# Two decoder layers: from a two-pass loop with barriers to one straight program, with the normalization folded into the product that turns x

## The chip, the cores and the metric

The kernel runs on one core of a Trainium2 chip. The metric is the device time of one execution in microseconds (us), the median of several runs. The engines are TensorE (PE, with its weight loads as PEld), VectorE (DVE), ScalarE (ACT), GpSimd (POOL) and SyncE (SP), which issues nearly all transfers.

## The reference

Two residual layers over x of 256 tokens by 1024 features, all in float32, and one closing normalization:

```
for l in range(2):
    h = x * rsqrt(mean(x*x) + 1e-6) * norm_g[l]
    proj = h @ w_in[l]                     # 1024 x 10008
    y_lru, y_s5, y_ret, y_nsa = four causal mixers of slices of proj
    ys = [y * silu(gate_path)]             # four times 256 x 512
    merged = sum(sigmoid(merge_n) * (ys_n @ w_branch[l, n]))
    x = x + merged @ w_out[l]
return x * rsqrt(mean(x*x) + 1e-6) * final_norm_g
```

The S5 mixer is a diagonal state-space recurrence. Its coefficients come from small per-layer parameter vectors by exponentials, sines and cosines, on tiles of 128x16.

## The kernel before

A layer is one list of 36 `CHUNKS`, each a product of 256 tokens with up to 512 output columns. The weights come in 74 units of two K-tiles through a ring of four tiles `raw` (`load_unit`, issued by SP). The twelve chunks named in `NATIVE` multiply `raw` in full float32, each such product leaving two records on PE. The others are split: ACT copies `raw` to `w_hi` (`cast_units`), POOL subtracts to `w_lo` (`split_lo`), and PE makes three products of rounded parts. The order of the work on every engine is written out by hand: PE calls `chunk(...)` and, in between, the small products of the mixers (`state_inputs(p)` and `state_outputs(p)` for the S5 mixer); DVE runs `angles(p)` and `scan_pair(p)` for the eight S5 pairs.

**Prologue** (L454 to L494). A block of its own: SP loads `x` whole, the constants, 13 small parameter rows (`load_vectors`) and two weight units. ACT makes the squares of x (`squares`, L438), DVE and POOL the inverse root `st[:, 2:4]` (`mean_square`, `inverse_root`), PE turns the parameter rows into columns (`turn_vectors`, L428) and DVE keeps them in `vec` (`keep_vectors`). The block ends with a barrier of all engines.

**Layer** (L496, a hardware loop of two passes). DVE scales x by the inverse root into `merged` (L844). PE transposes it in sixteen 128x128 pieces (L1322) into the bank tile `M`, ACT scales the pieces by `norm_g` into `h_full` and rounds `h_hi`, DVE subtracts `h_lo` (L863). Then comes the chunk `u_s5` (L1367). Meanwhile DVE and ACT work out the S5 coefficients (L846 to L909), which the tiles `b_exp` need (L914 to L918) before PE can turn them after `u_s5`. At the end `out_0a`, `out_1a`, `out_0b` and `last_chunk()` make the output product: DVE adds its parts to x (L1308, L1313), ACT squares them (L438) for the next normalization. The parameter rows of the next layer and its first two weight units are loaded and turned already here.

**Between the passes.** The block of the layer ends with a barrier, a block of its own clears all semaphores (`sem_clear`) and the loop jumps back.

**Epilogue** (L1716 to L1728). A third block: DVE multiplies x, inverse root and `final_norm_g` for each half of the tokens (L1727), SP stores each (L1721).

Of the kernel before, what the change touches and what calls it, by code (L numbers as in the profile page):

```python
# [65 lines left out]
N_FIRST = 2  # L66
# [4 lines left out]
SPLIT_UNITS = [u for u in range(NU) if CHUNKS[UNITS[u][0]][0] not in NATIVE]  # L71


def splits(upto):
# [7 lines left out]
    0, 8, 24, 28, 32, 36, 40, 44, 52, 68, 96, 112)  # L82

# [59 lines left out]
def hybrid_trunk(nc, a, out):  # L143
# [4 lines left out]
    with ctx:  # L148
# [3 lines left out]
        sems = []  # L152

        def sem(name):
            sems.append(ctx.enter_context(nc.semaphore(name)))
            return sems[-1]
# [43 lines left out]
        sc = sb("sc", [P, 7168])  # L200
        half_pi = sb("half_pi", [P, 1])
# [67 lines left out]
        x_loaded, const_loaded = (ctx.enter_context(nc.semaphore(n)) for n in ("x_loaded", "const_loaded"))  # L269
# [7 lines left out]
        x_norm, xT_done = sem("x_norm"), sem("xT_done")  # L277
# [30 lines left out]
        STAGE = ("vectors_loaded", "raw_first", "dt_rows", "vecT", "vec_ready", "sq", "msq", "var", "rstd", "g_loaded")  # L308
        nxt = {n: sem("next_" + n) for n in STAGE}
        first = {n: ctx.enter_context(nc.semaphore("first_" + n)) for n in STAGE}  # L310
        normed, stored = (ctx.enter_context(nc.semaphore(n)) for n in ("normed", "stored"))
# [3 lines left out]
        for u, (c, _, _, _) in enumerate(UNITS):  # L315
            if u >= N_FIRST:
                _count[u % N_RAW] += 32 if c == CHUNK["cmp"] else 16
            raw_target.append(_count[u % N_RAW])
# [79 lines left out]
        def load_vectors(sp, l, signal):  # L398

            def load(dst, src):  # L400
                sp.dma_start(dst, src).then_inc(signal, 16)

            for name, at, n in (("norm_g", V_NORM, 8), ("lru_conv_w", V_CONV, 16), ("lru_conv_b", V_CONVB, 4),
                                ("lru_ba", V_BA, 4), ("lru_bx", V_BX, 4), ("lru_lambda", V_LAM, 4), ("s5_d", V_D, 4),
                                ("s5_b_glu", V_BGLU, 8), ("s5_lambda_re", V_LR, 16), ("s5_lambda_im", V_LI, 16)):
                src = a[name][l]
# [7 lines left out]
            load(dt_in[V_DT:V_ROWS, :], a["s5_log_dt"][l].rearrange("(s g) -> s g", g=2))  # L414
            for m, name in enumerate(("nsa_pos_k", "nsa_pos_v")):
                load(rows2[16 * m:16 * m + 16, :], a[name][l].rearrange("(r s) d -> r (s d)", s=2))

        VECTORS_ALL, RAW_ALL = 16 * 13, 16 * N_FIRST

        def expand_dt(stage):  # L420

            nc.vector.tensor_copy(rows[V_DT:V_ROWS, :].rearrange("p (g n) -> p g n", g=2),
                                  bc(dt_in[V_DT:V_ROWS, :].unsqueeze(2), [16, 2, 64])).then_inc(stage["dt_rows"], 1)

        def turn_vectors(stage):

            for dst, src, n in ((M[:, 0, 0:V_ROWS], rows[0:V_ROWS, :], V_ROWS), (M[:, 0, P:P + 32], rows2[:, :], 32)):
                nc.tensor.transpose(dst, src, ident[0:n, 0:n]).then_inc(stage["vecT"], 1)  # L428

        def keep_vectors(stage):  # L430

            nc.vector.tensor_copy(vec[:, :], M[:, 0, 0:V_ROWS])
            nc.vector.tensor_copy(flat(pos[:, :, :]), M[:, 0, P:P + 32]).then_inc(stage["vec_ready"], 1)

        def squares(stage, half, t):

            e = slice(512 * half, 512 * half + 512)
            nc.scalar.activation(merged[:, t, e], x[:, t, e], ACT.Square,  # L438
                                 accum_out=st[:, 4 + 2 * half + t:5 + 2 * half + t]).then_inc(stage["sq"], 1)

        def mean_square(dve, stage):

            dve.wait_ge(stage["sq"], 2 * TT)
            nc.vector.tensor_tensor(st[:, 0:2], st[:, 4:6], st[:, 6:8], ALU.add).then_inc(stage["msq"], 1)
            dve.wait_ge(stage["msq"], 1)
            nc.vector.tensor_scalar(st[:, 0:2], st[:, 0:2], 1.0 / D, EPS, ALU.mult, ALU.add).then_inc(stage["var"], 1)

        def inverse_root(gp, stage):

            gp.wait_ge(stage["var"], 1)  # L450
            nc.gpsimd.tensor_tensor(st[:, 2:4], st[:, 0:2], m_half[:, 0:2], ALU.pow).then_inc(stage["rstd"], 1)


        with nc.Block() as block:  # L454
            @block.sync
            def _(sp):
                sp.dma_start(x[:, :, :], a["x"][0].rearrange("(t p) d -> p t d", p=P)).then_inc(x_loaded, 16)
                sp.wait_ge(first["dt_rows"], 1)
                sp.dma_start(const[:, :], a["constants"]).then_inc(const_loaded, 16)
                load_vectors(sp, 0, first["vectors_loaded"])  # L460
                for u in range(N_FIRST):
                    load_unit(sp, u, 0, first["raw_first"])
                sp.wait_ge(first["raw_first"], RAW_ALL)

            @block.gpsimd
            def _(gp):
                gp.memset(half_pi[:, :], math.pi / 2)
                gp.memset(m_half[:, :], -0.5)
                gp.memset(wa[:], 0.0)
                gp.memset(wx[:], 0.0)  # L470
# [5 lines left out]
            def _(act):  # L476
                act.wait_ge(x_loaded, 16)
                for half in range(2):
                    for t in range(TT):
                        squares(first, half, t)  # L480
# [1271 lines left out]
```

## Time and profile before

| | |
|---|---|
| median of 3 runs | 883.88 us (882.99 to 884.66) |
| the profiled execution, its own time | 883.38 us |
| its span, first to last instruction | 881.6 us |
| PE busy | 824.0 us, 93% of the span |
| PEld, DVE, ACT, POOL busy | 608.4, 562.3, 312.9, 313.7 us |
| mean granted TensorE clock | 0.973 of full speed |
| instructions | 10702 |

Busy times are those of one profiled execution. A line of the timeline says when a group of instructions starts and how long it takes; brackets behind it give how long the engine had been idle and what ended that.

### The profile page before, as it was taken

Reading aid. Unit: us, or ns where it says so; the run is one execution under the profiler, and the core shown is the slowest. Engines: PE = TensorE matmul, PEld = TensorE weight load, DVE = VectorE, ACT = ScalarE, POOL = GpSimd, SP = SyncE. Lnnn points to the kernel's source line nnn. Section 1 sums busy time; section 2 is a strip of 40 time slices with the busy share of each in tenths; the row PEclk is TensorE's granted clock in tenths of the full one; section 3 lists DMA queues with packets and bytes.
Section 4 is the critical chain, followed back from the end, with each engine's and each line's share of the span. In section 5 each row is a group of like instructions: output and inputs, shape, how many; then the busy total and the mean of one; then the engine's idle time right before and its main releaser. Section 6 shows DMA issues by size and latency. Waiting matters only on the chain. (4 is left out here: it accounts for less than half of the span.)

```text
span 881.6 us, 10702 instructions
## 1 busy us (share of the span) xinstructions
PE 824.0 (93%) x3852; PEld 608.4 (69%) x3852; DVE 562.3 (64%) x937; ACT 312.9 (35%) x519; POOL 313.7 (36%) x134
## 2 busy tenths in 40 slices
PE   4999989999999799999879998999998989999995
PEld 3874764446878688888768556744477777888884
DVE  3888999464697652634268889964928974445342
ACT  5310212013743445464334112110164544555441
POOL 0000000005568576668400000000057676666872
PEclk9999999999999899999979999999999998999998
DMA  7575524445345444454255745344453344444551
GB/s 227 135 240 152 184 84 140 122 146 189 116 120 168 120 143 144 144 168 147 69 113 150 236 137 191 96 143 128 136 190 122 117 140 127 138 137 154 168 167 71
DMA packets 87507, 128.29 MB, mean 146 GB/s; under 512 B 22204, under 2 KB 32792, under 8 KB 87320
## 3 DMA queue, kind: packets, MB, share of 16 engines
q1 hardware_dynamic: 87448, 127.55, 46.5%
q8 instruction: 32, 0.52, 0.2%
q14 instruction: 27, 0.22, 0.1%
HBM read 126.48 MB, written 1.05 MB: 145 GB/s over the span
## 5 line engine op out<-in xcount | busy, mean ns | idle before, releaser
L560 POOL TENSOR_TENSOR w_lo<-raw,w_hi 128x1024 fp32r<-128x1024 f32 x120 | 307.0, 2588 | 534.1 <-ACT w_hi L576 503.1
L1371 PE MATMUL proj<-raw,h_full 128*128 128x512 f32 (+1 forms) x512 | 213.2, 572 | 0.0
L1371 PEld LDWEIGHTS proj<-raw,h_full 128*128 128x128 f32 x512 | 95.7, 190 | 104.5 <-issue 100.6
L576 ACT ACTIVATE w_hi<-raw 128x1024 fp32r<-128x1024 f32 x120 | 122.5, 1050 | 65.1 <-DMA raw<-in_s_w_glu 27.1
L1327 PE MATMUL proj<-w_hi,h_hi 128*128 128x512 f32 x320 | 128.7, 402 | 0.9 <-POOL w_lo L560 0.9
L1367 PE MATMUL proj<-h_full,raw 128*128 128x256 f32 x512 | 119.0, 393 | 7.5 <-DVE gate L978 7.5
L1327 PE MATMUL proj<-w_lo,h_hi 128*128 128x512 f32 x320 | 125.0, 391 | 0.0
L1327 PE MATMUL proj<-w_hi,h_lo 128*128 128x512 f32 x320 | 125.0, 391 | 0.0
L1367 PEld LDWEIGHTS proj<-h_full,raw 128*128 128x128 f32 x512 | 100.2, 198 | 23.1 <-DVE gate L978 7.9
L1327 PEld LDWEIGHTS proj<-w_hi,h_hi 128*128 128x128 f32 x320 | 60.1, 188 | 14.3 <-issue 1.7
L1327 PEld LDWEIGHTS proj<-w_hi,h_lo 128*128 128x128 f32 x320 | 60.1, 188 | 13.0
L1327 PEld LDWEIGHTS proj<-w_lo,h_hi 128*128 128x128 f32 x320 | 60.2, 188 | 11.9 <-issue 0.5
L1327 PE MATMUL proj<-w_hi,ys_hi 128*128 128x512 f32 x128 | 53.3, 416 | 5.2 <-POOL w_lo L560 5.1
L1327 PE MATMUL proj<-w_hi,ys_lo 128*128 128x512 f32 x128 | 51.8, 405 | 0.0
L1327 PE MATMUL proj<-w_lo,ys_hi 128*128 128x512 f32 x128 | 51.6, 403 | 0.0
L576 ACT ACTIVATE sc<-sc,st 128x256 f32<-128x256 f32 x64 | 28.2, 442 | 57.2 <-DVE st L1249 57.2
L1002 DVE SCALAR_TENSOR_TENSOR mt<-mt,proj 128x1024 f32<-128x1024 f32 x12 | 14.7, 1221 | 39.3 <-PE proj L1327 39.3
L576 ACT ACTIVATE mt<-proj 128x1024 f32<-128x1024 f32 x16 | 16.3, 1019 | 63.3 <-PE proj L1371 54.4
L576 ACT ACTIVATE sc<-sc 128x512 f32<-128x512 f32 (+2 forms) x38 | 23.5, 666 | 42.0 <-DVE sc L1090 37.4
L1327 PEld LDWEIGHTS proj<-w_hi,ys_hi 128*128 128x128 f32 x128 | 25.3, 198 | 11.8 <-issue 5.9
L1327 PEld LDWEIGHTS proj<-w_lo,ys_hi 128*128 128x128 f32 x128 | 25.5, 199 | 5.1
L1327 PEld LDWEIGHTS proj<-w_hi,ys_lo 128*128 128x128 f32 x128 | 24.9, 195 | 5.7
(283 smaller groups left out, 1194.6 us busy)
## 6 DMA issues: line engine op xcount, KB each, us to landing
raw<-in_w_in SPq DMA_DIRECT2D x154, 512.0 KB, 3.5
raw<-in_w_branch SPq DMA_DIRECT2D x32, 512.0 KB, 3.6
raw<-in_w_out SPq DMA_DIRECT2D x16, 512.0 KB, 3.7
raw<-in_s_w_glu SPq DMA_DIRECT2D x8, 512.0 KB, 3.6
raw<-in_w_in SPq DMA_DIRECT2D x8, 256.0 KB, 2.5
merged<-in_nsa_ck_w SPq DMA_DIRECT2D x4, 512.0 KB, 5.7
mt<-in_nsa_ck_w SPq DMA_DIRECT2D x4, 512.0 KB, 6.8
merged<-in_nsa_cv_w SPq DMA_DIRECT2D x4, 512.0 KB, 5.1
```

Of the source, the lines that this page charges most:

```text
L560: nc.gpsimd.tensor_tensor(w_lo[:, s % N_SPLIT, 0:n * w], raw[:, u % N_RAW, 0:n * w], w_hi[:, s % N_SPLIT, 0:n * w].bitcast(f32), ALU.subtr ...
L576: i = nc.scalar.activation(out_, in_, func, **kw)
L1002: v.scalar_tensor_tensor(m, m, 1.0, src, ALU.add, ALU.mult).then_inc(evac(full), 1)
L1327: last = mm(dst, left[i], right[j], start=start and n == 0, stop=stop and n == 2, skip_group_check=True)
L1367: last = mm(ps[:, m * T:(m + 1) * T], rw[:, m * P:(m + 1) * P], h_full[:, k, :], start=st_ and m % 2 == 0, stop=sp_, skip_group_check=True)
L1371: last = mm(ps[:, 512 * t:512 * t + w], h_full[:, k, t * P:(t + 1) * P], rw, start=st_, stop=sp_, skip_group_check=True)
```

## The change

1. The loop becomes a Python loop: both layers are written out in one block, without a barrier, `sem_clear` or jump. `Layer` adds to every awaited count what a layer has signalled before (`PER_LAYER`). The closing normalization is in the same block.
2. The normalization of x is not done by DVE any more. `scaled_identity` makes a 128x128 matrix with the inverse root on its diagonal, and `turn_x` multiplies the pieces of x by it, a full float32 product in place of a transpose, for each half of the tokens by itself.
3. The inverse root is made for each half of the tokens by itself.
4. `parameters(l + 1)`, the S5 coefficients and other small preparations, run on DVE and ACT at the end of layer l. `turn_vectors` stands ahead of `out_1a` in place of behind it. In the first layer `parameters(0)` stands behind the eight `h_full` on ACT.
5. `h_hi` is made after `trig(0)`, `h_lo` after `gate_times("lru")`; PE waits for `h_lo` ahead of `merge_s5_1`.
6. At the start x is loaded in halves with the identity between them, then the parameter rows, seven issued by SP and six by ACT, then two weight units, the other constants and two more units. At the layer boundary all four first units of the next layer are loaded ahead, and the tables `b_nat` and `c_nat` after the last transposes of the layer.
7. The closing normalization is made and stored in four pieces of 512 columns.

The new helpers, the start of the block, and SP at the start:

```diff
+        def mean_of_first_half(dve, l, link):
+            Layer(dve, l).wait_ge(sq, TT if l else 2 * TT)
+            link(nc.vector.tensor_scalar(st[:, 0:2], st[:, 4:6], 1.0 / D, EPS, ALU.mult, ALU.add))
+        def mean_square(dve, l, t):
+            Layer(dve, l).wait_ge(sq, TT + t + 1)
+            nc.vector.scalar_tensor_tensor(st[:, t:t + 1], st[:, 6 + t:7 + t], 1.0 / D, st[:, t:t + 1],
+                                           ALU.mult, ALU.add).then_inc(var, 1)
+        def inverse_root(gp, l, t):
+            Layer(gp, l).wait_ge(var, t + 1)
+            nc.gpsimd.tensor_tensor(st[:, 2 + t:3 + t], st[:, t:t + 1], m_half[:, 0:1], ALU.pow).then_inc(rstd, 1)
+        def scaled_identity(dve, l, t):
+            Layer(dve, l).wait_ge(rstd, t + 1)
+            nc.vector.tensor_scalar(diag[:, t, :], ident, st[:, 2 + t:3 + t], None, ALU.mult).then_inc(diag_done, 1)
+        def turn_x(pe, l, t):
+            Layer(pe, l).wait_ge(diag_done, t + 1)
+            for k in range(KD):
+                at = (k % 2) * T + t * P
+                last = nc.tensor.matmul(M[:, k // 2, at:at + P], x[:, t, k * P:(k + 1) * P], diag[:, t, :], start=True, stop=True)
+                if t == TT - 1 and k % 2:
+                    last.then_inc(xT_done, 1)
...
-        with nc.Fori(0, DEPTH) as l:
-            with nc.Block() as block:
+        with nc.Block() as block:
+            for l in range(DEPTH):
...
+                    if l == 0:
+                        queue.dma_start(x[:, 0, :], a["x"][0][0:P, :]).then_inc(x_loaded[0], 16)
+                        queue.dma_start(const[:, 0:P], a["constants"][:, 0:P]).then_inc(ident_loaded, 16)
+                        queue.dma_start(x[:, 1, :], a["x"][0][P:T, :]).then_inc(x_loaded[1], 16)
+                        sp.wait_ge(cleared, 1)
+                        load_vectors(queue, 0, VECTORS_A)
+                        prefetch(0)
+                        prefetch(1)
+                        queue.dma_start(const[:, P:N_CONST], a["constants"][:, P:N_CONST]).then_inc(const_loaded, 16)
```

ACT at the start of a layer:

```diff
+                    if l == 0:
+                        scalar.wait_ge(cleared, 1)
+                        load_vectors(scalar, 0, VECTORS_B)
+                        for t in range(TT):
+                            scalar.wait_ge(x_loaded[t], 16)
+                            for half in range(2):
+                                squares(half, t)
+                    act.wait_ge(vec_ready, 1)
                     for k in range(KD):
                         if k % 2 == 0:
                             act.wait_ge(xT_done, k // 2 + 1)
                         run(h_full[:, k, :], M[:, k // 2, (k % 2) * T:(k % 2 + 1) * T], ACT.Copy, hfull_done,
                             scale=vec[:, V_NORM + k:V_NORM + k + 1])
-                        if k % 2:
-                            act.wait_ge(hfull_done, k + 1)
-                            run(flat(h_hi[:, k - 1:k + 1, :]), flat(h_full[:, k - 1:k + 1, :]), ACT.Copy, hhi_done)
+                    if l == 0:
+                        parameters(0)
```

ACT behind its last `cast_units`, and DVE behind the last `h_lo` of the layer:

```diff
+                    if l + 1 < DEPTH:
+                        parameters(l + 1)
...
+                    if l + 1 < DEPTH:
+                        keep_vectors(vector, l + 1)
+                        parameters(l + 1)
...
                     for t in range(TT):
                         dve.wait_ge(out_token, t + 1)
                         dst = x[:, t, 512:1024]
                         v.scalar_tensor_tensor(dst, pr("out_1b")[:, 512 * t:512 * t + 512], 0.25, dst,
                                                ALU.mult, ALU.add).then_inc(x_half, 1)
-                    mean_square(dve, nxt)
+                        if t == 0:
+                            mean_of_first_half(vector, l + 1, link)
+                            mean_square(vector, l + 1, 0)
+                    if l + 1 < DEPTH:
+                        scaled_identity(vector, l + 1, 0)
+                        mean_square(vector, l + 1, 1)
+                        scaled_identity(vector, l + 1, 1)
+                    else:
+                        final(0, 0)
+                        mean_square(vector, l + 1, 1)
+                        final(0, 1)
+                        final(1, 0)
+                        final(1, 1)
```

PE behind `last_chunk()`:

```diff
+                    if l + 1 < DEPTH:
+                        Layer(tensor, l + 1).wait_ge(vec_ready, 1)
+                        for t in range(TT):
+                            turn_x(tensor, l + 1, t)
```

## Rows read from the trace of the kernel before

**Rows 1.** The page, head and first part: busy time, share, instructions.

```profile
span 881.6 us, 10702 instructions
PE 824.0 (93%) x3852; PEld 608.4 (69%) x3852; DVE 562.3 (64%) x937; ACT 312.9 (35%) x519; POOL 313.7 (36%) x134
```

**Rows 2.** Waits of PE: waiting work <- releaser: us in total, times, longest.

```profile
PE M L1322 <- DVE merged L844: 11.0, 2, 8.7
```

**Rows 3.** Timeline around the layer boundary: start, us, engine, what.

```profile
438.02 0.39 PE L1327 MATMUL proj<-w_hi,h_lo 128*128 128x512 f32 x1
...
438.45 0.69 DVE L1313 SCALAR_TENSOR_TENSOR x<-proj,x 128x512 f32<-128x512 f32 x1 [2.03 <-PE proj L1327]
...
439.18 0.63 ACT L438 ACTIVATE merged<-x 128x512 f32<-128x512 f32 x1 [2.00 <-DVE x L1313]
...
440.37 0.70 POOL L451 TENSOR_TENSOR st<-st,m_half 128x2 f32<-128x2 f32 x1 [9.61 <-DVE st L446]
...
446.14 1.67 DVE L844 TENSOR_SCALAR merged<-x,st 128x512 f32<-128x512 f32 x4
...
447.08 3.67 PE L1322 MATMUL M<-const,merged 128*128 128x128 f32 x16 [8.67 <-DVE merged L844]
...
465.47 1.03 ACT L576 ACTIVATE u_s<-proj 128x1024 f32<-128x1024 f32 x1 [9.48 <-PE proj L1367]
```

**Rows 4.** Stretches: busy PE, PEld, DVE, ACT, POOL; granted clock; DMA share; GB/s.

```profile
449.00:450.00 1.00, 1.00 (x7) 1.00 (x6) 0.84 (x5) 0.97 (x4) 0.00 (x0) 0.50 0.72 172
453.00:454.00 1.00, 1.00 (x6) 0.90 (x5) 0.31 (x1) 0.97 (x3) 0.00 (x0) 1.00 1.25 144
```

**Rows 5.** Timeline of PE: one full float32 product, and two half chunks.

```profile
102.18 7.17 PE L1367 MATMUL proj<-h_full,raw 128*128 128x256 f32 x32
...
117.76 8.86 PE L1367 MATMUL proj<-h_full,raw 128*128 128x256 f32 x32 [3.74 <-DVE gate L978]
...
258.17 0.38 PE L1561 MATMUL M<-ret_v,sc 128*128 128x128 f32 x2
258.39 0.39 PE L1562 MATMUL M<-ret_v,sc 128*128 128x128 f32 x2
```

**Rows 6.** Timeline of the end.

```profile
871.93 0.69 DVE L1313 SCALAR_TENSOR_TENSOR x<-proj,x 128x512 f32<-128x512 f32 x1 [2.03 <-PE proj L1327]
...
876.02 2.48 DVE L1727 SCALAR_TENSOR_TENSOR merged<-x,st,kd 128x1024 f32<-128x1024 f32 x2 [2.25 <-PEq L1710]
```

**Rows 7.** Timeline of the start.

```profile
0.74 1.28 ACT L438 ACT_TABLE_LOAD   x1 [0.74 <-PEq L1743]
...
5.60 0.63 ACT L438 ACTIVATE merged<-x 128x512 f32<-128x512 f32 x1 [3.57 <-DMA x<-in_x]
...
6.96 0.42 SPq L401 DMA_DIRECT2D rows<-in_nsa_pos_v  x1
...
10.44 0.22 DVE L422 COPY rows<-dt_in 16x128 f32<-16x128 f32 x1 [1.89 <-DMA rows<-in_nsa_pos_v]
...
13.80 3.67 PE L1322 MATMUL M<-const,merged 128*128 128x128 f32 x16 [2.33 <-DVE merged L844]
...
17.27 14.78 PE L1367 MATMUL proj<-h_full,raw 128*128 128x256 f32 x64
```

**Rows 8.** A stretch of the start, in the columns of rows 4.

```profile
15.00:16.00 1.00, 1.00 (x7) 1.00 (x6) 0.86 (x6) 0.97 (x3) 0.00 (x0) 1.00 0.95 338
```

**Rows 9.** Timeline of DVE: three waits, and the parameters of the second layer.

```profile
143.41 0.69 DVE L943 TENSOR_TENSOR sc<-M,sc 128x512 f32<-128x512 f32 x1 [1.59 <-PE M L1327]
...
427.35 0.28 DVE L432 COPY vec<-M 128x112 f32<-128x112 f32 x1 [3.45 <-PE M L428]
...
433.01 1.23 DVE L1308 SCALAR_TENSOR_TENSOR x<-proj,x 128x1024 f32<-128x1024 f32 x1 [5.29 <-PE proj L1327]
...
447.74 0.15 DVE L846 SCALAR_TENSOR_TENSOR small<-vec 128x4 f32<-128x4 f32 x1
...
458.73 0.17 DVE L909 TENSOR_TENSOR small<-small 128x16 f32<-128x16 f32 x1
```

More of the change, by code:

```diff
@@ L65 @@
 N_RAW = 4
-N_FIRST = 2
 N_SPLIT = 5
@@ L405, in load_vectors @@
                                 ("s5_b_glu", V_BGLU, 8), ("s5_lambda_re", V_LR, 16), ("s5_lambda_im", V_LI, 16)):
+                if name not in names:
+                    continue
                 src = a[name][l]
@@ L425, in turn_vectors @@
[L425 to L435, printed above, removed]
+                if name in names:
+                    load(rows2[16 * m:16 * m + 16, :], a[name][l].rearrange("(r s) d -> r (s d)", s=2))
@@ new lines, in turn_vectors, with keep_vectors @@
+        def turn_vectors(pe, l):
+            Layer(pe, l).wait_ge(dt_rows, 1)
+            at = vectors_at(l)
+            for dst, src, n in ((at[:, 0:V_ROWS], rows[0:V_ROWS, :], V_ROWS), (at[:, P:P + 32], rows2[:, :], 32)):
+                nc.tensor.transpose(dst, src, ident[0:n, 0:n]).then_inc(vecT, 1)
+        def keep_vectors(dve, l):
+            Layer(dve, l).wait_ge(vecT, 2)
+            at = vectors_at(l)
+            nc.vector.tensor_copy(vec[:, :], at[:, 0:V_ROWS])
+            nc.vector.tensor_copy(flat(pos[:, :, :]), at[:, P:P + 32]).then_inc(vec_ready, 1)
@@ L437, in squares @@
+        def squares(half, t):
             e = slice(512 * half, 512 * half + 512)
             nc.scalar.activation(merged[:, t, e], x[:, t, e], ACT.Square,
[L439 to L446, printed above, removed]
@@ L637, in _ @@
                     run(cT[:, :, :, :].rearrange("p f q n -> p (f q n)"), MF[:, 0:1024], ACT.Copy, bcT_ready)
-                    cast_units(UNIT_END[CHUNK["u_s5"]] + N_SPLIT)
                     trig(0)
+                    act.wait_ge(hfull_done, KD)
+                    for k in range(0, KD, 2):
+                        run(flat(h_hi[:, k:k + 2, :]), flat(h_full[:, k:k + 2, :]), ACT.Copy, hhi_done)
                     next_cast("cmp")
@@ new lines, in _ @@
+                    if l == 0:
+                        mean_of_first_half(vector, 0, link)
+                        for t in range(TT):
+                            mean_square(vector, 0, t)
+                        expand_dt(vector, 0)
+                        vector.wait_ge(ident_loaded, 16)
+                        for t in range(TT):
+                            scaled_identity(vector, 0, t)
+                        keep_vectors(vector, 0)
+                        parameters(0)
+                        vector.wait_ge(const_loaded, 16)
@@ L1046, in _ @@
                     gate_times("lru")
+                    for k in range(0, KD, 2):
+                        dve.wait_ge(hhi_done, k // 2 + 1)
+                        v.tensor_tensor(flat(h_lo[:, k:k + 2, :]), flat(h_full[:, k:k + 2, :]),
+                                        flat(h_hi[:, k:k + 2, :]).bitcast(f32), ALU.subtract).then_inc(hlo_done, 2)
                     dve.wait_ge(evac("ck"), ev("ck"))
```

354 lines of the change are left out of this document (180 added, 174 removed).

## The prediction

> **What bounds the kernel now.** I read the busy times first: TensorE is busy 824.0 of 881.6 us [rows 1]. So PE's own sequence sets the time, and only PE's 57.6 idle us, or PE running slowly, can be won. The waits of PE come next. The longest is that of the transposes of x for DVE's scaled x, 11.0 us in two places, 8.7 of them in one [rows 2]. Then the timeline of the layer boundary, where the 8.7 sit. The last product of layer 0 ends at 438.4; DVE adds it to x from 438.45 to 439.14, ACT squares at 439.18, POOL makes the inverse root from 440.37 to 441.07, and then nothing happens until DVE scales at 446.14: 5.1 us of barrier, clearing of semaphores and jump. PE starts at 447.08 with 16 transposes and finishes `u_s5` at about 465.4, just before ACT reads it [rows 3]. The granted clock there is 0.50, the 1.2 GHz level, and is back at 1.00, the 2.4 GHz level, by 453 [rows 4]. Inside the layers the same view shows the cost of such a drop: a half chunk takes 7.17 us, and 8.86 behind a wait of 3.74 us [rows 5].
>
> Both layers take the same time from the end of `u_s5` to DVE's last addition: 438.45 - 32.05 = 406.4 and 871.93 - 465.4 = 406.5 us [rows 3, 6, 7]. The change leaves that stretch nearly alone, so I cost three places: start, boundary, end.
>
> **The boundary.** DVE's last addition to x is at 438.45 as before, ended at 439.14, and ACT's square follows. Between that square and POOL stood two small operations of DVE; now it is one, as the first halves are summed ahead. I take 0.2 us off: POOL from 440.2 to 440.9 [rows 3]. `scaled_identity` is not in the trace; a DVE operation on 128x512 takes 0.69 us [rows 3], so one on 128x128 lies between 0.15 (the smallest, [rows 9]) and 0.69. I take 0.3 with its signals: 441.3. Now PE: the same piece of x costs two records in place of one. Two records take 258.39 - 258.17 = 0.22 us at full clock [rows 5], so eight pieces 1.8 us. `turn_x` of the first tokens needs the first diagonal, which DVE makes right behind 439.14; it runs from about 439.4 to 441.2 and hides under squares and root. The second half runs from 441.3 to 443.1. Each ACT scaling is ready long before PE gets to its K-tile, as before. PE is idle for 1.0 us in place of 8.67, so I let the clock stay up. `u_s5` is 64 records; 32 take 7.17 with the tail, about 7.05 back to back [rows 5], so 14.1: end at 457.2 in place of 465.4. Gain 8.2 us. If the clock fell nevertheless, the eight pieces would cost 3.7 (16 records at 3.67 per 16, [rows 3]) and `u_s5` some 0.7 more: gain 5.7. If diagonal and signals cost nothing: 8.5.
>
> **What the boundary is moved on to.** `keep_vectors` and `parameters(1)` now stand on DVE ahead of the additions to x. Before, DVE was idle 5.29 us ahead of 433.01, and 3.45 us ahead of the copies of `keep_vectors` at 427.35. In the second layer the parameters run from 447.74 to 458.9, 11.2 us, but in this stand four `h_lo` and a memset, 3.7 us together: 7.5 remain [rows 9]. The earlier `turn_vectors` lets the copies begin at 427.35 - 3.45 = 423.9; they take 0.4, and 7.5 us on is 431.8, and 433.01 is when DVE is needed: 1.2 us of room, and as PE only needs x after 438.4, a small overrun is hidden by `last_chunk` also. On ACT the exponentials and the table load stand between its last casts and the squares, in idle time. The loads of the four units and of `b_nat` and `c_nat` come earlier on SP, and the parameter rows pass nothing new. All at zero.
>
> `h_hi` and `h_lo`: ACT's four roundings move under the chunk `cmp`, where ACT waits. DVE's four subtractions (2.6 us) fall on the S5 stage, where DVE is solidly busy. Next behind them is `scan_pair(6)`, ahead of which DVE waits 1.59 us for PE [rows 9]. So it comes 1.0 us later, and PE asks for its result a whole half chunk (7 us) later. Zero, between 0 and 2.6 us per layer. Their old place was not on the path either: PE was busy with `u_s5`.
>
> **The end.** DVE adds at 871.93, root at the same distance as before, now at about 874.4. Before, the final products start at 876.02, two of 1.24 us, ending at 878.50, and the span ends 3.1 us later with the store [rows 6]. Now the first piece (0.62 us) runs during ACT's square, the second during the root, the last two from 874.4 to 875.65. With the same 3.1 us: 878.75 in place of 881.6, gain 2.8 us. Bounds, by estimate: 2.4, if the issues of three stores ahead of it hold up the last by 0.4, and 3.4, if a store of half the size lands 0.6 sooner.
>
> **The start.** Two paths meet: squares to root to diagonals, and parameter rows. ACT first issues six loads at 0.42 us [rows 7], from about 1.0 to 3.5, then loads its table, 1.28, then four squares at 0.62: 7.3 (before it waited for x until 5.60). DVE and POOL: 0.6 for three operations, 0.7 for the root, 0.3 for the diagonal, and PE starts at 9.0. The last parameter row was issued at 6.96 and used at 10.44, 3.5 us later [rows 7]; now the seventh of SP goes out at about 4.2, so 7.7: no longer late. Now the clock. The transposes at the start take 3.67 us for 16 records, exactly as at the boundary [rows 3, 7], where the clock is 0.50, yet the clock row of the start says 1.00 [rows 8]. I believe the durations. The first half of `turn_x` then costs 3.7, until 12.7; if the clock rises as at the boundary, where it was still 0.50 3 us after PE's start and 1.00 6 us after it [rows 3, 4], at 14, the second costs 1.3 slow and 1.1 fast: 15.1. `turn_vectors`, the copies and the first `h_full` now stand behind it: 1.5 us by estimate, less than the 3.4 between 10.44 and 13.80, which hold more. So `u_s5` starts at 16.6, at full clock, and ends at 30.7 in place of 17.27 + 14.78 = 32.05 [rows 7]. Gain 1.3. If the rows come at 10.44 as before and all stays slow: 11.0 + 7.3 + 1.5 + 14.1 = 33.9, a loss of 1.8. If the clock rises at 12 and the squares come 0.5 sooner: gain 2.8. DVE's parameters now wait for ACT behind all eight `h_full`, but by my estimate they and `b_exp` are done before `u_s5` is, with about 1 us to spare.
>
> The Trainium skill ("TensorE: Matmul & The Clock Gate", section "What's actually happening") says that the default state is the throttled one and activity releases it, and warns that records of the throttle can be unreliable; the duration agrees with it, the clock row does not. By the clock row alone, both halves would cost 3.5 us in all and the start's gain would be 3.2.
>
> The Trainium skill ("DMA: Bandwidth & Descriptors", section "Issuing engines are not separate DMA queues") says that a second issuing engine only saves issue time. By that the six loads on ACT save 2.5 us of issue on SP, which is what I count.
>
> **Sum.** 1.3 + 8.2 + 2.8 = 12.3 us. The profiled execution: span 881.6 becomes 869.3, its own time 883.38 becomes 871.1. The median stands 0.5 above it: 871.6.
>
> **Rivals.** (a) The start gives back what it got: a double-cost product at the slow clock, behind loads, and the columns of the parameters behind it. Gain 5.7 to 9.5 us with a boundary short too: about 876. For it: the slow transposes [rows 7]. Against: the parameter rows, the last thing waited for at 10.44, are issued 2.8 us sooner. (b) The S5 stage pays for `h_lo`: 2.6 us per layer and, if PE stops for 3.7 us again, 1.7 for the clock as in [rows 5]; up to 8.6 in all, 880. Against: the wait of 1.59. (c) Slower than before: written out, the layer's instructions no longer come from a loop, and PE starves for them in layer 1. It decides once that costs 12.3 us, 3% of 406; at 4% the time would be 888. Against: the first pass came from fresh code too, and took the same 406.4. (d) More is won, as the S5 stage of layer 1 starts with `angles(0)` ready: it would have to shorten the 3.74 us wait [rows 5], but DVE waits for PE before it; with the clock 5 us, 866.
>
> **Chances.** Forecast, 869.2 to 874: 0.74. (a) 0.13, (b) 0.07, (c) 0.03, (d) 0.03. The three places at their bounds give 883.9 - 14.7 = 869.2 and 883.9 - 6.3 = 877.6; leaving out the far ends of (b), (c) and (d) I take 868.5 to 876.5. A change within 0.2% (1.8 us) is what this kernel's measurement can't tell from none. Faster 0.96, within 0.01, slower 0.03.
>
> **What would show it.** The profile after should have: no wait of PE above 2 us at the boundary, and the clock at 1.00 through it; `u_s5` of layer 1 ending 18.8 us after DVE's last addition in place of 27.0; DVE's parameters done before its addition of `out_0b`; the stretch from `u_s5` to the last addition still at 406.4; `u_s5` of layer 0 starting at 16 to 17; and 6.8 us from the last addition to the end in place of 9.7. Wrong would be a new wait of PE between `gate_lru` and `ret_q`, or a first product later than 10 us.

## The result, and the profile after

The kernel after takes 872.87 us (median of 4 executions, 872.72 to 873.78) against 884.27 us for the kernel before on the same chip (4 executions, 882.99 to 884.96): a ratio of 0.9875, 95% interval 0.9858 to 0.9892. The forecast was 871.6 us in a range of 868.5 to 876.5. Run again in the last series, unchanged, it took 871.24 us (5 executions, 870.41 to 873.03) against 885.73, ratio 0.9845 (0.983 to 0.986).

The page's head, against [rows 1]:

```profile
span 871.2 us, 10151 instructions
PE 825.7 (95%) x3882; PEld 610.6 (70%) x3882; DVE 563.3 (65%) x935; ACT 312.3 (36%) x519; POOL 315.7 (36%) x137
```

PE has the same work to within 2 us (30 records more: two for each piece of x in place of one would be 32 more), and the span is 10.4 us shorter: idle time was won, as the argument wanted it. The waits of PE:

```profile
PE M L517 <- DVE diag L510: 11.6, 2, 9.6
...
PE proj L1470 <- DVE gate L1056: 7.3, 2, 3.7
```

The first row looks like the old one [rows 2], and isn't: its 9.6 are the start, where PE has nothing to do yet, and at the boundary only 2.0 are left of 8.67. The other row, inside the layers, is not new: PE waited 3.74 us for `gate` before too [rows 5]. So the account is made by places. "Stretch" is from ACT's first reading of `u_s5` to the end of PE's last output product.

| us in the profiled execution | before | after | won | forecast |
|---|---|---|---|---|
| start: ACT reads `u_s5` of layer 0 | 32.08 | 31.80 | 0.28 | 1.3 |
| stretch of layer 0 | 406.33 | 406.63 | -0.30 | 0 |
| boundary: PE's last product to ACT reading `u_s5` | 27.06 | 19.66 | 7.40 | 8.2 |
| stretch of layer 1, to DVE's last addition | 406.46 | 406.52 | -0.06 | 0 |
| end: from that addition on | 9.67 | 6.59 | 3.08 | 2.8 |
| span | 881.6 | 871.2 | 10.4 | 12.3 |

This is one execution of each kernel. In the second profiled execution of the kernel after, layer 0's stretch was 405.75 us and layer 1's 406.05, so differences of some 0.5 to 0.9 us in a stretch are not read as an effect.

The boundary after, in the timeline, against [rows 3] (PE's last product of layer 0 ends at 438.43):

```profile
439.25 0.68 DVE L1404 SCALAR_TENSOR_TENSOR x<-proj,x 128x512 f32<-128x512 f32 x1
...
439.96 0.63 ACT L488 ACTIVATE merged<-x 128x512 f32<-128x512 f32 x1 [0.90 <-DVE x L1404]
...
440.43 3.81 PE L517 MATMUL M<-diag,x 128*128 128x128 f32 x32 [2.00 <-DVE diag L510]
440.96 0.55 POOL L505 TENSOR_TENSOR st<-st,m_half 128x1 f32<-128x1 f32 x1 [1.00 <-DVE st L499]
441.54 0.29 DVE L510 TENSOR_SCALAR diag<-const,st 128x128 f32<-128x128 f32 x1 [0.66 <-POOL st L505]
...
444.07 1.25 PE L1470 MATMUL proj<-h_full,raw 128*128 128x256 f32 x5
```

What to see: the 5.1 us of nothing are gone, the diagonal of the first tokens is made before POOL has the second root, and 32 products take 3.81 us where 16 transposes took 3.67, because the granted clock stays at 1.00, the 2.4 GHz level, where it was 0.50 [rows 4]. The window of the products:

```profile
440.00:443.00 3.00, 2.57 (x23) 2.60 (x24) 1.74 (x6) 0.69 (x3) 0.55 (x1) 1.00 0.04 7
```

From DVE's last addition to ACT reading `u_s5` (458.09) there are 18.84 us; 18.8 was forecast. But the addition comes at 439.25, 0.82 us behind PE's product; before, it came 0.04 behind. Those 0.8 are the whole miss of the boundary. What DVE did ahead of it, and what POOL did at that time:

```profile
424.24 1.89 DVE L919 SCALAR_TENSOR_TENSOR small<-vec 128x4 f32<-128x4 f32 x1
426.05 0.16 DVE L920 TENSOR_SCALAR small<-vec 128x8 f32<-128x8 f32 x1
426.13 2.37 DVE L921 TENSOR_SCALAR small<-vec 128x4 f32<-128x4 f32 x1
...
428.49 2.37 DVE L924 TENSOR_TENSOR small<-vec,small 128x16 f32<-128x16 f32 x1
430.89 0.17 DVE L925 TENSOR_TENSOR small<-small 128x16 f32<-128x16 f32 x1
...
435.86 1.23 DVE L1399 SCALAR_TENSOR_TENSOR x<-proj,x 128x1024 f32<-128x1024 f32 x1
```

```profile
423.70 7.13 POOL L622 TENSOR_TENSOR w_lo<-raw,w_hi 128x1024 fp32r<-128x1024 f32 x3 [3.36 <-ACT w_hi L640]
```

Three of the smallest operations that DVE has take 1.89 to 2.37 us, each to the end of one of POOL's three subtractions of some 2.4; the others take 0.16 or 0.17. So `parameters(1)` takes 11.6 us (424.24 to 435.82), not 7.5; `out_0b` is added at 435.86 in place of 433.01, 2.85 us late, and 0.8 of that reaches the boundary.

The start after, against [rows 7]:

```profile
3.40 0.44 ACTq L436 DMA_DIRECT2D rows<-in_nsa_pos_v  x1
3.87 1.28 ACT L488 ACT_TABLE_LOAD   x1 [3.87 <-issue]
...
9.57 6.75 PE L517 MATMUL M<-diag,x 128*128 128x128 f32 x32 [9.57 <-DVE diag L510]
...
17.71 14.05 PE L1470 MATMUL proj<-h_full,raw 128*128 128x256 f32 x64 [1.12 <-ACT h_full L640]
```

PE begins at 9.57 (9.0 forecast), but its 32 products take 6.75 us, 0.21 each, nearly all at the slow pace. The same kernel run again took 5.61 us for them, began `u_s5` at 16.49 instead of 17.71, and had a span of 868.6. The same window of the start in the two executions, the first run above:

```profile
13.50:14.50 1.00, 1.00 (x7) 1.00 (x6) 0.00 (x0) 0.00 (x0) 0.00 (x0) 1.00 1.22 294
...
13.50:14.50 1.00, 1.00 (x12) 1.00 (x11) 0.00 (x0) 0.00 (x0) 0.00 (x0) 1.00 1.19 308
```

PE makes 7 records in it in the one and 12 in the other, and the clock row says 1.00 in both. In the first the pace is 6 to 7 records in each us until 15.5, in the second it has risen by 13.5. And the end, against [rows 6]:

```profile
864.61 0.69 DVE L1404 SCALAR_TENSOR_TENSOR x<-proj,x 128x512 f32<-128x512 f32 x1 [1.01 <-PE proj L1431]
865.22 0.74 DVE L1394 SCALAR_TENSOR_TENSOR merged<-x,st,kd 128x512 f32<-128x512 f32 x1
...
866.17 0.75 DVE L1394 SCALAR_TENSOR_TENSOR merged<-x,st,kd 128x512 f32<-128x512 f32 x1
866.33 0.99 POOL L505 TENSOR_TENSOR st<-st,m_half 128x1 f32<-128x1 f32 x1 [2.10 <-DVE st L499]
867.36 1.41 DVE L1394 SCALAR_TENSOR_TENSOR merged<-x,st,kd 128x512 f32<-128x512 f32 x2 [0.44 <-POOL st L505]
```

One of the four final pieces runs ahead of the last root and one beside it. Beside that one the root takes 0.99 us, in this and in all other profiles of the changed kernels, where at the boundary it takes 0.55: here DVE's instruction makes POOL's longer.

### The profile page after: what moved, and what is told of

It is laid out like the page before. It is cut to its first block, busy times and chain, and to the rows that moved or that the text cites. A ratio compares the mean times of both kernels' runs of the same rounds, so it can differ in the third digit from the quotient of the medians.

```text
span 871.2 us, 10151 instructions
## 1 busy us (share of the span) xinstructions
PE 825.7 (95%) x3882; PEld 610.6 (70%) x3882; DVE 563.3 (65%) x935; ACT 312.3 (36%) x519; POOL 315.7 (36%) x137
## 4 chain that ended last, share of the span: by engine, by line
PE 55%; issue 29%; DVE 8%; POOL 5%; ACT 1%; DMA 1%; POOLq 0%; DVEq 0%; SPq 0%; ACTq 0%
PE proj L1431 27%; PE proj L1474 11%; POOL w_lo L622 5%; PE proj L1470 5%; PE M L1426 3%; PE M L1731 1%; PE M L1736 1%; DVE sc L1315 1%; PE M L1701 1%; PE M L1755 1%; PE M L1754 1%; PE M L517 1%; PE M L1753 1%; PE M L1431 1%; PE M L1572 1%
```

## The experiments

Three questions were open: what held DVE ahead of the additions, what the start costs and why, and which part of the change wins what. Each kernel is the one after with the edit shown. The medians of before beside them were 883.75 us for the first four, 883.35 for the next four and 885.73 for the last three, so medians are compared within a series, and places by the profiled execution. The kernel after stands beside others in the last series only. Its two ratios are 0.9875 and 0.9845, and of the eight kernels of the first two series only the one with the halves of h back, 0.994, lies clear of both.

| kernel | median us (lowest to highest) | ratio to before, 95% interval | `u_s5` 0 begins | stretch 0 | last addition late by | boundary |
|---|---|---|---|---|---|---|
| after | 872.87 (872.72 to 873.78) | 0.9875 (0.9858 to 0.9892) | 17.71 | 406.6 | 0.82 | 19.7 |
| parameters late | 870.71 (870.48 to 871.95) | 0.9854 (0.9835 to 0.9873) | 16.77 | 406.1 | 0.04 | 18.7 |
| short subtractions | 872.02 (870.47 to 873.61) | 0.9872 (0.9852 to 0.9891) | 16.53 | 405.8 | 0.04 | 18.7 |
| filler products | 870.53 (869.23 to 872.03) | 0.9854 (0.9831 to 0.9877) | 14.60 | 406.3 | 0.81 | 19.7 |
| vectors first | 871.26 (870.06 to 872.46) | 0.9862 (0.9841 to 0.9883) | 14.71 | 406.8 | 0.80 | 19.6 |
| transposes back | 873.36 (871.45 to 873.88) | 0.9885 (0.9869 to 0.9902) | 15.18 | 406.9 | 0.81 | 20.5 |
| barrier back | 873.04 (871.79 to 874.03) | 0.9875 (0.9855 to 0.9895) | 16.46 | 408.5 | 0.81 | 20.9 |
| halves of h back | 878.44 (877.21 to 879.63) | 0.994 (0.992 to 0.9961) | 17.23 | 412.6 | 0.81 | 19.7 |
| combined | 869.39 (866.99 to 871.53) | 0.9847 (0.9825 to 0.9868) | 13.14 | 406.0 | 0.03 | 18.7 |
| after, again | 871.24 (870.41 to 873.03) | 0.9845 (0.983 to 0.986) | 16.49 | 405.8 | 0.81 | 19.7 |
| first layer transposed | 869.01 (867.75 to 869.55) | 0.9811 (0.9797 to 0.9824) | 13.38 | 406.5 | 0.04 | 18.7 |
| combined, again | 869.88 (867.39 to 871.37) | 0.9825 (0.9807 to 0.9842) | 13.12 | 406.3 | 0.04 | 18.7 |

The end was 6.5 to 6.6 us in all of them.

**Parameters late.** The parameters of layer 1 stand again in layer 1, on DVE and on ACT.

```diff
-                        if l == 0:
-                            parameters(0)
+                    parameters(l)
...
                         keep_vectors(vector, l + 1)
-                        parameters(l + 1)
```

> The S5 parameters of layer 1 go back to the start of layer 1 (DVE behind its diagonals, ACT behind the eight h_full); their rows are still turned and kept under the output product. Theory (POOL's w_lo subtractions hold DVE's small operations with two inputs, so the parameters took 11.6 us in place of 7.5 and pushed the additions to x back): out_0b is added at about 433 in place of 435.9, the last addition comes at about 438.4 in place of 439.25, u_s5 of layer 1 ends at 457.2 in place of 458.0, and the time is 0.8 us less, about 872.1. Rival 1 (the parameters were late for their own length, and nothing behind them depends on it): the same 872.9. Rival 2 (they are needed early): b_exp comes after u_s5 and PE waits for it, slower by 1 to 3 us.

The last addition is on time again and the boundary takes 18.73 us, 0.93 less. So at the boundary moving them was a loss of 0.9 us. Not all of it is won in the end: layer 1's stretch is 406.7 to 407.4 us in the five profiles with the short boundary (this kernel, the next, the combined one twice and the one with the first layer transposed) and 405.7 to 406.7 in the seven others with the change, on average some 0.5 us longer. What gives that back isn't shown. Nor does this run say yet whether the parameters are too many, or too slow.

**Short subtractions.** The last three `w_lo` of layer 0 are made over 8 columns, so that POOL is done with each at once; what these pieces give to the output products is left out.

```diff
-   nc.gpsimd.tensor_tensor(w_lo[:, slot(s, l), 0:n * w], raw[:, u % N_RAW, 0:n * w], ...
+   m = 8 if l == 0 and s >= len(SPLIT_UNITS) - 3 else n * w
+   nc.gpsimd.tensor_tensor(w_lo[:, slot(s, l), 0:m], raw[:, u % N_RAW, 0:m], ...
```

> POOL's last three w_lo subtractions of layer 0 cover 8 columns in place of 1024; the rest of those three tiles keeps the values of earlier units, so that part of the split product is left wrong. Everything else is as in the changed kernel. Theory (POOL's subtraction holds DVE): the small operations of the parameters that took 1.89 and twice 2.37 us take 0.17 as at the start, the parameters end near 431 in place of 435.8, the addition of out_0b is back at 433 and u_s5 of layer 1 ends 0.8 us sooner. Rival (DVE was slow there for another reason: ACT, the loads on SP, an instruction that is fetched): the long operations stay 1.9 to 2.4 us, and nothing moves.

DVE's timeline, the same instructions as above (L920 is L919 of the kernel after, and so on):

```profile
422.27 0.16 DVE L920 SCALAR_TENSOR_TENSOR small<-vec 128x4 f32<-128x4 f32 x1
...
422.43 0.16 DVE L922 TENSOR_SCALAR small<-vec 128x4 f32<-128x4 f32 x1
...
424.25 0.17 DVE L925 TENSOR_TENSOR small<-vec,small 128x16 f32<-128x16 f32 x1 [1.59 <-ACT small L641]
...
431.13 1.22 DVE L1400 SCALAR_TENSOR_TENSOR x<-proj,x 128x1024 f32<-128x1024 f32 x1 [1.75 <-PE proj L1432]
```

With POOL out of the way the three take 0.16, 0.16 and 0.17, all parameters 7.1 us (422.27 to 429.38, a wait for ACT of 1.59 in it), DVE waits 1.75 us for PE ahead of `out_0b`, and the boundary is 18.73. So the 7.5 us and the 1.2 us of room of the forecast were right for DVE alone, and POOL's subtractions are what made it late. The median hardly shows it: executions spread by 3 us here. The start, which comes next, varies by itself, but it isn't all of the spread: the combined kernel, whose start is the same in both of its profiles, spreads as far.

**Filler products.** PE makes 20 products of zeros from 1 us on, extra work that nobody reads.

```diff
+                        tensor.wait_ge(zeros, 1)
+                        for _ in range(20):
+                            mm(proj[0][:, 0:P], cols(0, P), cols(0, P), start=True, stop=True)
                         tensor.wait_ge(ident_loaded, 16)
```

> 20 float32 products of a zeroed 128x128 tile on PE before the first diagonal is there. Theory (turn_x of layer 0 took 6.75 us for 32 records because PE was at the 1.2 GHz level, whatever the clock row says): the products run slowly for about 5 us, turn_x then takes 3.5 to 4.5, u_s5 starts at 14.5 to 15.5 in place of 17.7, and the time falls by 2 to 3 us, to about 870.3. Rival (turn_x is slow for its operands or for the loads that run at the same time): turn_x still takes 6.7 us and the time is the same.

PE's timeline of the start:

```profile
1.05 6.70 PE L1532 MATMUL proj<-sc 128*128 128x128 f32 x40 [1.05 <-DVE sc L956]
9.40 3.81 PE L518 MATMUL M<-diag,x 128*128 128x128 f32 x32 [1.65 <-DVE diag L511]
...
14.60 1.75 PE L1472 MATMUL proj<-h_full,raw 128*128 128x256 f32 x7 [1.12 <-ACT h_full L641]
```

The 32 products with the diagonal take 3.81 us, exactly what they take at the boundary, in place of 6.75. Their operands are the same, and so are the loads beside them (413 to 451 GB/s between 9 and 11 us, 378 to 420 in the kernel after), so neither made them slow: what PE did before sets the pace of these products. The filler brings `u_s5` forward by 1.9 to 3.1 us against the two executions of the kernel after.

**Vectors first.** In layer 0 the vectors are turned ahead of x, and DVE copies them between its two diagonals.

```diff
-                        for t in range(TT):
-                            turn_x(tensor, 0, t)
                         turn_vectors(tensor, 0)
+                        for t in range(TT):
+                            turn_x(tensor, 0, t)
```

> In layer 0 PE turns the parameter rows before the products that turn x, and DVE keeps them between the two diagonals. Theory (u_s5 waited for vec: two records, two copies and the first h_full stood behind turn_x): vec is there before turn_x ends, PE's wait of 1.1 us for h_full is gone, u_s5 starts at about 16.4 in place of 17.7 and the time falls by about 1.3 us, to 871.6. Rival (the parameter rows come late and now hold turn_x): PE's first work is later than 9.6 and nothing is won.

PE turns them at 8.60, when it has nothing else, starts on x at 9.31, and the wait of 1.12 us for `h_full` is gone:

```profile
8.60 0.66 PE L476 MATMUL proj<-const,rows 112*128 112x112 f32 x2 [8.60 <-DVE rows L468]
9.31 5.56 PE L517 MATMUL M<-diag,x 128*128 128x128 f32 x32
14.71 1.46 PE L1470 MATMUL proj<-h_full,raw 128*128 128x256 f32 x6
```

So the tail behind x, turning, copying and the first `h_full` (1.5 us in the forecast, 1.55 in the kernel after, from 16.16 to 17.71), need not be there at all.

**Transposes back.** Both layers scale x on DVE and transpose it, all else as after.

```diff
-   nc.vector.tensor_scalar(diag[:, t, :], ident, st[:, 2 + t:3 + t], None, ALU.mult)
+   nc.vector.tensor_scalar(merged[:, t, :], x[:, t, :], st[:, 2 + t:3 + t], None, ALU.mult)
...
-   nc.tensor.matmul(M[...], x[:, t, k * P:(k + 1) * P], diag[:, t, :], start=True, stop=True)
+   nc.tensor.transpose(M[...], merged[:, t, k * P:(k + 1) * P], ident)
```

> DVE scales each half of x by its inverse root into merged (one operation of 128x1024) and PE turns it by transposes, 16 records in place of 32; all else is the changed kernel. Theory (the product costs two records of PE for each piece, and is worst at the slow clock): at the start turn_x takes 3.5 us in place of 5.6 to 6.8, DVE's scaling costs 0.4 us more than a diagonal, so u_s5 starts 2 to 2.5 us sooner; at the boundary PE's second half takes 0.9 in place of 1.8 us and DVE costs 0.4 more, 0.5 sooner. Together 2.5 to 3 us less, about 870. Rival (the product is what made the boundary short): last addition to the end of u_s5 grows from 18.8 us by 1 us or more and the time is 873 to 875.

PE's timeline at the start and at the boundary, and a window of the latter:

```profile
10.19 3.60 PE L517 MATMUL M<-const,merged 128*128 128x128 f32 x16 [10.19 <-DVE merged L510]
...
438.60 1.06 PE L517 MATMUL M<-const,merged 128*128 128x128 f32 x8 [2.46 <-DVE merged L510]
440.06 1.81 PE L517 MATMUL M<-const,merged 128*128 128x128 f32 x8 [0.39 <-DVE merged L510]
```

```profile
440.00:443.00 3.00, 2.94 (x12) 2.67 (x13) 2.76 (x9) 2.31 (x7) 0.00 (x0) 0.54 0.00 0
```

At the boundary the transposes begin later (DVE's scaling is 0.75 us, the diagonal 0.29) and PE waits twice; the first eight take 1.06, the next eight 1.81, and the clock is 0.54 in the window where it was 1.00. PE's records take 2.87 us in place of 3.81, and yet the boundary is 0.9 us longer. All of that is the clock's: PE begins `u_s5` 5.5 us after its last product of layer 0 (5.6 in the kernel after), and then `u_s5` takes 15.0 us until ACT reads it, where it takes 14.0. At the start it is the other way round: 3.60 us in place of 5.43 to 6.75. So the product with the diagonal is a gain of 0.9 us at the boundary, where its shorter waits leave the clock up, and a loss of 1.3 to 2.5 (15.18 against 16.49 and 17.71) at the start, where the pace is slow with either form. The median of this kernel, in another series, doesn't tell the sum of the two from nothing.

**Barrier back.** The only edit is that each layer is a block of its own again, with the barrier that ends it; normalization stays ahead of it, and the loads of the first weight units of layer 1 stand at the end of layer 0.

```diff
-        with nc.Block() as block:
-            for l in range(DEPTH):
+        for l in range(DEPTH):
+            with nc.Block() as block:
```

> Each of the two written-out layers is a block of its own, so one barrier of all engines stands between them, without a jump and without clearing of semaphores. The first four weight units of layer 1 are loaded ahead of the barrier as before; turn_x is in front of it, the eight h_full behind it. Theory (of the 7.4 us won at the boundary most was jump, clearing and the second barrier): the barrier alone holds h_full by about 1 us and lets it begin only when turn_x is over: 1.5 to 2.5 us slower than the changed kernel, about 874.5, and PE's idle time behind turn_x about 2 us. Rival (the barrier itself is the 5 us): PE idle 5 us or more, the clock falls to 0.50, and the time is 879 or more.

PE's timeline: 

```profile
441.07 3.81 PE L517 MATMUL M<-diag,x 128*128 128x128 f32 x32 [1.99 <-DVE diag L510]
445.86 4.34 PE L1470 MATMUL proj<-h_full,raw 128*128 128x256 f32 x19 [0.98 <-ACT h_full L640]
```

ACT makes its first `h_full` 4.17 us after PE begins with x (445.24), without the barrier 2.56; 0.98 of it reaches PE. The boundary is 20.87 us, 1.2 longer. So of the 7.4 us a bare barrier, with work on both sides of it, is 1.2 in this profile; the median, in another series, doesn't show it. The other 6.2 belong to what went with it: the clearing of semaphores, the jump, the scaling behind them and the clock that fell meanwhile. The run with the transposes back puts 0.9 us on the form of the product; the rest was not taken apart. This kernel also lost 1.9 us inside layer 0, ahead of the barrier. DVE's timeline there:

```profile
240.85 2.44 DVE L1204 TENSOR_TENSOR sc<-u_s,const 128x128 f32<-128x128 f32 x1
...
250.50 0.29 DVE L1208 TENSOR_TENSOR u_s<-sc 128x128 f32<-128x128 f32 x1
```

and POOL's and PE's:

```profile
240.70 9.62 POOL L622 TENSOR_TENSOR w_lo<-raw,w_hi 128x1024 fp32r<-128x1024 f32 x4 [4.46 <-ACT w_hi L640]
...
244.28 0.39 PE L1431 MATMUL proj<-w_lo,ys_hi 128*128 128x512 f32 x1
...
251.05 1.15 PE L1426 MATMUL M<-const,u_s 128*128 128x128 f32 x8 [2.04 <-DVE u_s L1209]
```

Four operations of 128x128 take 2.44 to 2.48 us each beside POOL's four subtractions, and 0.29 right behind them. They do so in the kernel after too (2.45 at 241.10), where PE waits 0.46 us for them and here 2.04. DVE isn't slower here; PE comes sooner, for in the kernel after it makes eight products at 0.63 us each ahead of this wait, behind its wait of 2.55 us for `w_lo`:

```profile
244.64 0.63 PE L1431 MATMUL proj<-w_lo,ys_hi 128*128 128x512 f32 x1
```

Here all of them take 0.39 or 0.40, and the products at 0.63 us come behind the wait of 2.04. The slow stretch is the same; ahead of the wait DVE's operations hide it, behind it they don't. That is 0.9 of the 1.9 us. The other 1.0 was lost earlier, between 86 and 190 us after ACT reads `u_s5`, and stays open. The kernel with the first layer transposed, below, has no barrier and waits 2.1 us at this place of layer 1, so the barrier isn't the cause. Small operations of DVE held by POOL's subtractions, as ahead of the boundary, here set the time at which PE goes on.

**Halves of h back.** `h_hi` and `h_lo` are made where they were, behind `h_full`.

```diff
                         vector.wait_ge(const_loaded, 16)
+                    for k in range(0, KD, 2):
+                        dve.wait_ge(hhi_done, k // 2 + 1)
+                        v.tensor_tensor(flat(h_lo[:, k:k + 2, :]), flat(h_full[:, k:k + 2, :]), ...
```

> h_hi stands again between the h_full on ACT, and h_lo at the start of DVE's layer, in place of inside the S5 stage. Theory (both places lie beside other work): the same time as the changed kernel, 872.9 within 1 us, scan_pair(6) comes 1 us sooner and PE gains nothing. Rival (the h_lo in the S5 stage costs PE time): 1 to 5 us faster, with PE's waits in 110 to 170 us smaller. Second rival (at the start of the layer they delay b_exp): slower by 1 to 3 us, with a wait of PE behind u_s5 of layer 0.

DVE's timeline and PE's in layer 0:

```profile
27.48 0.17 DVE L952 TENSOR_TENSOR small<-small 128x16 f32<-128x16 f32 x1
27.74 2.50 DVE L967 TENSOR_TENSOR h_lo<-h_full,h_hi 128x512 fp32r<-128x512 f32 x4
```

```profile
17.23 14.05 PE L1470 MATMUL proj<-h_full,raw 128*128 128x256 f32 x64 [1.12 <-ACT h_full L640]
34.66 3.21 PE L1426 MATMUL M<-const,sc 128*128 128x128 f32 x16 [3.38 <-DVE sc L1000]
```

Layer 0 is 6 us longer, layer 1 (406.69) isn't. DVE's parameters of layer 0 now end at 27.65 because they wait behind ACT's `h_full`; with 2.5 us of `h_lo` on top, the matrices that PE needs at 31.3 are ready at 34.5, PE stops for 3.38 us and runs slowly behind that (16 records in 3.21 us, where they take 1.91 at full clock). That is the second rival's place, at twice its size. So the move of `h_lo` costs the S5 stage nothing that the stretches show (406.63 and 406.52 after, 406.33 and 406.46 before), and the rest of the change can't do without it in layer 0. Whether it would win anything in the kernel before wasn't run.

**Combined.** Parameters late, vectors first and filler products together.

> The edits of the runs with late parameters, with parameter rows turned first, and with PE warmed together. Theory (they act in three different places: boundary, the wait behind turn_x, turn_x itself): u_s5 of layer 0 starts at about 13.3, the last addition of layer 0 follows PE's last product at once, and the time is 3.5 to 5 us below the changed kernel, 868 to 869. Rival (with u_s5 starting so soon DVE's parameters and b_exp of layer 0 or layer 1 come too late): PE waits 1 to 3 us behind u_s5 for b_exp, and only 2 us are won.

The boundary has its 18.7 us and `u_s5` begins at 13.14, the span is 865.2.

**The last series**, with five rounds: the kernel after, the combined one, and one in which the start's lesson is used without extra work: parameters late, vectors first, and x transposed in layer 0 alone.

```diff
+            if l == 0:
+                nc.vector.tensor_scalar(merged[:, t, :], x[:, t, :], st[:, 2 + t:3 + t], ...
+            else:
                 nc.vector.tensor_scalar(diag[:, t, :], ident, st[:, 2 + t:3 + t], ...
```

> The kernel after, unchanged, as the yardstick for the two others of this call. Every theory expects its first median of 872.87 us within 1 us, and a ratio to the kernel before of 0.9875 within 0.0015. It also tells how much the start varies by itself: if u_s of layer 0 is read at a time more than 0.5 us from 31.80, the 0.3 us that the start gained in the first profiled execution is not a size to rely on.

> The parameters at the place in layer 1 where they were, the vectors turned first, and in layer 0 alone x scaled by DVE and transposed, as before; layer 1 keeps the product with the diagonal. No extra products. Theory: at the start TensorE runs slowly whatever it does, so 16 slow records instead of 32 save 1.8 us or more there, while at the boundary the product is the better form. u_s of layer 0 begins by about 13.5 us without a wait, the boundary takes 18.7 us, and the median is 1 to 3 us under the kernel after of this call. Rival: DVE's two scalings of 0.75 us each and their signals eat what the fewer records save, and the start is that of the run with vectors first, 14.7 us: then only the 0.9 us of the boundary remain.

> The combined kernel again, beside the kernel after on the same chip with more rounds. If its first result was right, its median is 2 to 4.5 us under that of the kernel after in this call, with intervals of the two ratios to the kernel before that do not overlap, u_s of layer 0 begins at 13 to 14 us, and the boundary takes 18.7 us. If it was luck of single executions, the difference is under 1.5 us.

The kernel after moved by 1.6 us in its median, and its start by 1.2 us: more than I gave it. The one with the first layer transposed is 2.2 us under it, and their intervals (0.9797 to 0.9824, 0.983 to 0.986) don't meet: it is faster than the kernel before and than the kernel after. Its places came as expected:

```profile
8.72 0.66 PE L476 MATMUL proj<-const,rows 112*128 112x112 f32 x2 [8.72 <-DVE rows L468]
9.91 3.68 PE L521 MATMUL M<-const,merged 128*128 128x128 f32 x16 [0.52 <-DVE merged L511]
13.38 15.10 PE L1473 MATMUL proj<-h_full,raw 128*128 128x256 f32 x64
```

But `u_s5` takes 15.10 us in place of 14.05: the slow stretch is passed in it instead. ACT reads it at 28.52, against 28.73 with the vectors first and all of x as products, so the sixteen records fewer win 0.2 us in these two profiles and not the 1.8 of the theory; what the rival said of the start is nearer. So most of the 2.2 us are likely those of the parameters and the vectors; a kernel with these two edits alone wasn't run. The combined kernel was 1.4 us under the kernel after, which is less than the 2 I had asked for, with intervals that overlap; its profiled spans are the shortest (865.2 and 865.6), but its executions spread over 4 us. That it is faster than the kernel after is likely and not shown.

## Why the prediction was right, and where it was not

- **PE's idle time at the boundary is what can be won.** Right: 7.4 of the 10.4 us. PE's wait ahead of x went from 8.67 to 2.0 us, against the 1.0 forecast, of which 0.8 is the late addition, and the clock stayed up. From DVE's last addition on, 18.84 us were measured and 18.8 forecast.
- **"7.5 remain", "1.2 us of room ... a small overrun is hidden by `last_chunk` also".** This is the step that failed. `parameters(1)` was sized at 7.5 us from rows of layer 1, where POOL is idle, and was moved under POOL's subtractions, where it takes 11.6. The 4.1 us more used up DVE's room of 1.2 us and what `last_chunk` hides, and 0.8 us came through. The trace of before had the sign in it: the copy of `rows` on 16x128, 0.22 us at 10.44 [rows 7], takes 2.29 us at 411.33, under POOL's `w_lo`. Its row:

```profile
411.33 2.29 DVE L422 COPY rows<-dt_in 16x128 f32<-16x128 f32 x1
```

  Durations were taken from the place where the work was, not from where it went. The Trainium skill ("SBUF — State Buffer", section "Who interferes with whom") says that VectorE and GpSimd share a pair of ports, that a VectorE instruction with two inputs in SBUF or in a two-port mode takes it, and that the later of the two engines is blocked to the end of the other's instruction. The trace agrees: 1.89 and 2.37 us, each ending with one of POOL's. That the `TENSOR_SCALAR` of 2.37 us is in such a mode, no run here shows.
- **The start: 1.3 us.** 0.3 in the first profiled execution, 1.5 in the second of the same kernel. Six profiles have this start (the kernel after twice, parameters late, short subtractions, barrier back, halves of h back): the same 32 records take 5.43 to 6.75 us, and ACT reads `u_s5` 0.3 to 1.5 us sooner than before. So 1.3 lies inside, and the first execution is the worst of the six. The belief in durations against the clock row was right: the pace is slow until some 13 to 16 us under a clock row of 1.00, where the forecast had 14. A point stood where a range was due. The warning on records of the throttle that the prediction takes from the Trainium skill ("TensorE: Matmul & The Clock Gate") stands in that page's section "Seeing it yourself", and the trace agrees with it: 1.00 under 32 records in 6.75 us, 3.81 at full clock. By the clock row alone the prediction's own terms give 9.0 + 3.5 + 1.5 + 14.1 = 28.1, a gain of 3.9 and not the 3.2 that it says; with the filler, at full clock, `u_s5` was read at 28.69, a gain of 3.4. The first product came 0.6 us later than forecast: ACT's six loads ran until 3.84 and not 3.5, and its four squares took 2.7 us (5.17 to 7.90) and not 2.5.
- **The end: 2.8 us.** 3.1, from two misses that partly cancel. The last root takes 0.99 us beside DVE's final piece and not 0.70, so the final pieces end 4.2 us after the last addition and not 3.7; but the store, half as large, ends 2.4 us behind them and not 3.1, which the prediction had as a bound.
- **The stretches stay.** 406.6 and 406.5 against 406.3 and 406.5, so rivals (b) and (c) fell: the subtractions of `h_lo` in the S5 stage cost nothing, and written out, layer 1 ran as fast as from the loop. Rival (d) fell too: the wait for `gate` is still 3.6 to 3.7 us. Of rival (a) the start's part came in the first execution, 1.0 of the 1.3 us given back, and not in the second. As a ratio to the kernel before, the forecast was 871.6 / 883.88 = 0.9861, between the two that were measured, 0.9875 and 0.9845. It is nearer to them than the start's variation lets one forecast, so part of the nearness is luck.
- **"Their old place was not on the path either."** True of the kernel before and of layer 1, false beside the other edits: 6 us in layer 0.

**Open.** How the other 6.2 us of the boundary divide between the jump, the clearing and the scaling behind them; what decides when the clock rises at the start; and what makes layer 1 some 0.5 us longer behind a shorter boundary.

## What to carry to other kernels

Work that is moved under other work takes the durations of its new neighbours: look in the trace for an operation that already runs there, and compare it with itself elsewhere. PE's start is priced by its number of records, its boundaries by its waits, so the form that wins in one place can lose in the other. A move that wins nothing alone can be what makes room for the next one, so parts should be undone one at a time from the changed kernel as well as costed from the old one.

## What the runs showed of the hardware

- A DVE instruction of 0.16 us took 2.37, and one of 0.29 took 2.48, while POOL subtracted 128x1024 from SBUF to SBUF; with POOL's at 8 columns (0.20 us) the first took 0.16. The other way round, POOL's root over one column took 0.99 us in place of 0.55 beside a DVE instruction on 128x512.
- The clock row read 1.00 from 10 to 16 us while 32 products took 6.75 us; 40 records of zeros ahead of them made it 3.81. Without these the same products took 5.43 to 6.75 us over six executions.
- A barrier between two blocks with work on both sides cost the boundary 1.2 us in one profile.
